# Long convolution: VectorE rounds a weight chunk behind a group's products instead of ahead of them

## What is computed

```python
def fft_long_conv(u, spec):
    L = u.shape[1]
    U = jnp.fft.rfft(u.astype(jnp.float32), n=2 * L, axis=1)
    return jnp.fft.irfft(U * spec, n=2 * L, axis=1)[:, :L].astype(u.dtype)
...
    for o in range(HY_ORDER):        # two orders
        z = gates[o] * (fft_long_conv(z, spec[:, o]) + z * bias[o])
    return (z * jax.nn.silu(gate)) @ w_out
```

## Time and profile before

| | |
|---|---|
| median of 3 runs | 1955.11 us |
| the profiled execution | 1956.08 us |
| its span, first to last instruction | 1954.3 us |
| TensorE busy | 1907.5 us, 98%, 9606 matmuls |
| VectorE busy | 1392.6 us, 71% |
| ScalarE busy | 834.9 us, 43% |
| GpSimd busy | 230.6 us, 12% |
| mean granted TensorE clock | 0.993 |

### The profile page before, as it was taken

How to read it: one execution, slowest core, us unless ns; L and a number is a source line. 1 busy time by engine, 2 the same in 40 slices (tenths; PEclk the granted TensorE clock), 3 DMA queues, 4 the chain that set the end, 5 groups by cost and what they waited for, 6 DMA issues and landing times.

```text
span 1954.3 us, 24352 instructions
## 1 busy us (share of the span) xinstructions
PE 1907.5 (98%) x9606; PEld 1600.1 (82%) x9606; DVE 1392.6 (71%) x2099; ACT 834.9 (43%) x1332; POOL 230.6 (12%) x233
## 2 busy tenths in 40 slices
PE   7999999999999999999999999999999989999997
PEld 6888888788888888888888888778888878888886
DVE  5477766998899579758756874555655568888884
ACT  5333434542233357644323443454434444554542
POOL 2133321002201310010000001000000101001011
PEclk9999999999999999999999999999999989999998
DMA  5211213346444431134353332311111323332421
GB/s 187 76 60 64 65 54 108 135 142 227 170 169 144 157 100 41 47 129 140 135 177 117 143 108 93 109 57 44 33 44 33 119 66 128 98 130 85 151 89 54
DMA packets 60530, 206.55 MB, mean 106 GB/s; under 512 B 6784, under 2 KB 7232, under 8 KB 59264
## 3 DMA queue, kind: packets, MB, share of 16 engines
q1 hardware_dynamic: 52864, 191.36, 29.2%
q10 hardware_dynamic: 7552, 13.64, 2.0%
HBM read 194.48 MB, written 10.49 MB: 105 GB/s over the span
## 4 chain that ended last, share of the span: by engine, by line
PE 85%; DVE 9%; ACT 3%; issue 2%; POOL 1%; DMA 0%; DVEq 0%; SPq 0%; ACTq 0%
PE PS L335 22%; PE PS L339 22%; PE PS L338 22%; PE PS L448 2%; PE PS L954 2%; DVE wlo L1901 2%; PE PS L342 2%; PE PS L346 1%; PE PS L345 1%; PE PS L746 1%; PE PS L943 1%; ACT whi L1221 1%; PE PS L727 1%; PE PS L397 1%; DVE tmp_h L2733 1%
## 5 line engine op out<-in xcount | busy, mean ns | idle before, releaser
L335 PE MATMUL PS<-nhi,whi 128*128 128x512 f32 x1456 | 585.7, 402 | 14.7 <-DVE nlo L1938 3.4
L339 PE MATMUL PS<-nhi,wlo 128*128 128x512 f32 x1456 | 569.1, 391 | 0.0
L338 PE MATMUL PS<-nlo,whi 128*128 128x512 f32 x1456 | 568.2, 390 | 0.0
L1901 DVE TENSOR_TENSOR wlo<-raw,whi 128x1024 fp32r<-128x1024 f32 x288 | 364.4, 1274 | 163.7 <-ACT whi L1221 162.2
L1221 ACT ACTIVATE whi<-raw 128x1024 fp32r<-128x1024 f32 x288 | 300.8, 1052 | 166.9 <-PE PS L335 109.3
L335 PEld LDWEIGHTS PS<-nhi,whi 128*128 128x128 f32 x1456 | 274.4, 188 | 75.1 <-issue 9.7
L339 PEld LDWEIGHTS PS<-nhi,wlo 128*128 128x128 f32 x1456 | 273.8, 188 | 59.2
L338 PEld LDWEIGHTS PS<-nlo,whi 128*128 128x128 f32 x1456 | 274.6, 189 | 51.1 <-issue 1.0
L2810 POOL TENSOR_TENSOR diag<-diag,sqb 128x512 f32<-128x512 f32 (+1 forms) x56 | 73.8, 1318 | 750.2 <-ACT sqb L1230 667.0
L335 PE MATMUL PS<-hh_f,whi 128*128 128x512 f32 x352 | 137.2, 390 | 0.0
L338 PE MATMUL PS<-hl_f,whi 128*128 128x512 f32 x352 | 137.0, 389 | 0.0
(11 more groups left out here) (373 smaller groups left out, 3287.7 us busy)
## 6 DMA issues: line engine op xcount, KB each, us to landing
raw<-in_stream SPq DMA_DIRECT2D x288, 512.0 KB, 3.5
aw_f<-in_ada SPq DMA_DIRECT2D x48, 512.0 KB, 4.5
rows<-sd_f ACTq DMA_DIRECT2D x32, 256.0 KB, 2.4
rows_h<-rows SPq DMA_DIRECT2D x8, 1024.0 KB, 6.0
wd_f<-in_decay ACTq DMA_DIRECT2D x16, 256.0 KB, 3.2
hT<-in_xT SPq DMA_DIRECT2D x8, 256.0 KB, 7.1
out<-hT SPq DMA_DIRECT2D x8, 256.0 KB, 2.0
wd_f<-in_filt_out ACTq DMA_DIRECT2D x8, 128.0 KB, 2.9
```

The lines of the kernel that those rows point to most:

```text
L335: op = e.matmul(out, hi, xh, start=first, stop=False)
L338: e.matmul(out, hi, xl, start=False, stop=False)
L339: return e.matmul(out, lo, xh, start=False, stop=last)
L1901: e.tensor_tensor(m.wlo[:, c % HL, :], m.raw[:, c % RAW, :], m.whi[:, c % HL, :].bitcast(F), SUB).then_inc(*s.w_lo.tick(c))
```

## The change

In VectorE's program, the calls of `w.tiles` for a forward group stand behind the sum of the products (line 2705) and ahead of y_lo, where before they stood ahead of the products. The four calls at the head of f0 stay in their place. Nothing else differs; the other engines' programs are the same.

```diff
@@ -2686,8 +2686,6 @@
                     q.wait_ge(*s.made_a.at("hm", od, c))
                     e.tensor_tensor(a.hl[0:1, 0, 0, :], a.hm[0:1, :], a.hh[0:1, 0, 0, :].bitcast(F),
                                     SUB).then_inc(*s.made_v.tick("hm", od, c))
-                for _ in range(Z_TILES[j] + (2 if j == 0 else 4)):
-                    w.tiles(1)
                 q.wait_ge(*s.filled.at("bu", od, c, j))
                 q.wait_ge(*s.taken_a.at("bk", od, c, j))
                 if j:
@@ -2703,6 +2701,8 @@
                 e.tensor_tensor(tmp[:, 3, :], bi, kx, MUL).then_inc(*s.taken_v.tick("bi", od, c, j))
                 q.wait_ge(*s.taken_v.at("bi", od, c, j))
                 e.tensor_tensor(tmp[:, 2, :], tmp[:, 2, :], tmp[:, 3, :], ADD).then_inc(*s.made_v.tick("spec", od, c, j))
+                for _ in range(Z_TILES[j] + (2 if j == 0 else 4)):
+                    w.tiles(1)
                 for p in range(2):
                     q.wait_ge(*s.made_a.at("y_hi", od, c, j, p))
                     e.tensor_tensor(y.lo[:, i, p, :], tmp[:, 2 * p, :], y.hi[:, i, p, :].bitcast(F),
```

## The result

The changed kernel takes 1966.43 us (median of 4 runs, 1965.07 to 1968.90), the one before 1955.43 (4 runs, 1955.07 to 1959.74). The ratio is 1.0050, 95% interval 1.0034 to 1.0067: slower by 9.8 us, 6.6 to 13.1. The difference of the medians is 11.0. The forecast was 1962.3, range 1958.6 to 1966.0, on top of a kernel before at 1955.11; 1955.11 + 9.8 = 1964.9 is inside the range, and the median as it stands, 1966.43, is 0.4 above it.

The account below looks back on a forecast made before the run. The prediction took TensorE's chain of waits as the bound (85% of the span). Convolution terms -1.04, +1.37, +6.43 and +0.47 sum to +7.2 us: 1956.08 to 1963.3, less 0.97 to the run median, 1962.3; range 1958.6 to 1966.0.

Parts of the forecast that it names:

- Which chunks move and when TensorE needs them: Convolutions: 13 roundings move, three of 16 groups have none in the loop; each chunk's first-read tile is named.
- B: Second of four convolutions: one 2.40 us stall ahead of its third forward group, old waits gone, +1.37 us in all.
- C: Third convolution: three stalls of 0.94, 2.64 and 2.55 us, no old wait removed; +6.43 us with restarts.
- D: Fourth convolution: first inverse step -0.30 us, two stalls of 1.26 and 1.11, old waits gone; +0.47 us in all.
- A: First convolution: first inverse step starts earlier, -1.04 us; seventh tile of its last forward group covered by only 0.1.
- The step from the sum to the rounding: VectorE, sum's start to rounding's start: taken as 0.62 us; upper bound would add 0.23 to each of six stalls.
- What is removed: VectorE's wait ahead of the products for ScalarE's half of the chunk: 11.5 us idle, mostly costing TensorE nothing.
- Queues: SyncE's raw-chunk loads: buffers freed 1 to 4 us later, 11 us of work in hand; cost nothing, at most 4 us.
- A granted clock below 1.00: Sign in the third convolution that would show the forecast wrong, as would no wait for `wlo` there.
- Rival 3: TensorE's clock falls after stalls in the third convolution: one fall +10.3 us, time 1965.4; two 1968.5; chance 0.08.
- Rival 1: Gains alone: moved chunks cost nothing, only removed waits count across the convolutions; -4.3 us, time 1950.8; chance 0.06.
- Rival 2: Stalls partly absorbed behind the third convolution, at half its 6.4 us: +4.0 us, time 1959.1; chance 0.17.

Follow-up runs that it names:

- filled kernel: The changed kernel with ten unused matmuls in each of three long waits for a late chunk; +9.0 us against the kernel before, median 1965.4 us.
- placement by deadline: Against the kernel before, rounding late only in the seven groups whose chunk TensorE needs later than VectorE has it; -3.3 us (-5.1 to -1.6).

## Why the prediction came out as it did

**Which chunks move and when TensorE needs them**: right. All six forecast stalls stand in the trace at the tile that was named, and no seventh. As slips (idle + 0.16): B 2.45 (forecast 2.40), C 0.97, 2.64, 2.57 (0.94, 2.64, 2.55), D 1.38, 1.14 (1.26, 1.11). The seventh tile of f3 in A, with 0.1 to spare, did not wait.

**The step from the sum to the rounding**, bounded in the forecast between 0.60 and 0.85, is 0.61.

**What is removed**: A -1.04 as forecast. The waits for `bu` and y_lo that were to go are gone, and the two of i0 that were to stay stayed. i0 of D gained 0.20, not 0.30: it came at 1881.24, where 1870.17 + 11.27 = 1881.44 would be no gain.

**Queues**: no wait for a load appears. SyncE's queue waits for roundings 12.5 us at the longest, and nobody waits for it.

**The clock** is the step that failed in size: a fall behind a long wait was put at nothing in the main sum. "A granted clock below 1.00" in C was one of the forecast's own signs of being wrong, and it came: 0.79 in 1814 to 1822. Rival 3 had the mechanism, a chance of 0.08 and 3.1 us a fall; the main sum had none. In the runs it came behind 9 of 13 such waits, 1.7 us each, so the three long waits of the changed kernel are worth 3 x 9/13 x 1.7 = 3.5 us on average. 7.2 + 3.5 = 10.7, where 9.8 (interval 6.6 to 13.1) and, the second time, 12.7 (9.6 to 16.0) were measured. With 12.7 the time would have been above the range, so that it lies in the range is in part luck. I had taken one wait of 2.07 us that kept the clock for the case; in the 14 traces of this study the same wait (2.05 to 2.09 us) is followed by a fall in seven. The 3.1 us came from a stretch in which the clock stayed down for longer. That the falls make up the difference is shown for the profiles by the stretch from i0 of A to i0 of D, with and without them. For the time it is made likely by the filled kernel's 3.7 us; the intervals overlap, so the size of that is open.

**Rival 1** (gains alone) is wrong for the change, but it is what the placement by deadline gives: -3.3 where -4.3 was its sum. **Rival 2** (part absorbed) is wrong: nothing of C's lateness was regained behind it. The 1.1 us regained behind D lies in the output stage, where the clock's fall came near 1942 us before and 1956 after, while TensorE still worked in the former; it has nothing to do with the rounding.

## What to carry to other kernels

An operand that one engine prepares in program order has a deadline at its consumer: write down for each the tile at which it is first read and compare it with the finish time at the new place, group by group, since the phase of chunks against groups decides and the same edit gains in one place and costs in another. Put such work where its engine waits for the consumer anyway, here between the first product and the second, and look at what runs beside it on GpSimd if it reads two operands from SBUF, and at what the other engines wait for behind it (here the sum). Price a TensorE wait of two microseconds or more with the chance of a fall of the clock on top.

## What the runs showed of the hardware

- A wait of TensorE of 1.7 to 2.5 us between dense work is often, but not always, followed by 3 to 4 us at the 1.2 GHz level, 1.7 us lost: behind 9 of 13 waits of 2.2 to 2.5 us, 7 of 14 of 2.05 to 2.09, and behind 1.96, 1.87 and 1.73 us, but not behind 1.86, 1.84, 1.79, 1.70 and 1.67. The same wait of the same kernel does it in one execution and not in the next (2.48 us in C), so a kernel with several such waits has a spread, here 1965.4 to 1973.3; the kernel before, which has one such wait in this stage, has 1953.9 to 1960.4 on the same chip. The Trainium skill, page "TensorE: Matmul & The Clock Gate", section "HAM oscillation — how this bites in real kernels", describes how idling between bursts of matmuls brings the half clock again and again; the traces agree, with waits that are shorter than those of the page's example.
- A subtraction of 128 x 1024 with both inputs in SBUF takes 1.22 us alone and 1.92 to 1.94 when it starts 0.4 us into a GpSimd subtraction of 1.27 to 1.30 us, which is not slowed (13 groups of one run).
